# Last routing unit of a two-block transformer kernel: four V rows added by VectorE, buffers taken in another order, next weights loaded and split one block sooner

## The reference, cut to what matters

```
x[t] += sum over heads h and choices k of  gate[t,h,k] * gelu(xn[t] . U[idx[t,h,k]]) * V[idx[t,h,k]]
```

## Time and profile before

| | us |
|---|---|
| median of three runs | 1544.4 |
| lowest, highest run | 1544.03, 1548.16 |
| the profiled execution | 1549.62 |
| its span on the core | 1547.8 |
| TensorE busy in the span | 1387.3 |
| VectorE busy | 1032.8 |
| ScalarE busy | 707.7 |
| GpSimd busy | 622.3 |
| HBM read | 409.93 MB, 268 GB/s over the span |

### The profile page before, as it was taken

The page is one execution under the profiler, slowest core; times in us unless marked ns, Lnnn a source line. Parts: engine busy times, 40 slices in busy tenths (PEclk is TensorE's granted clock), DMA queues, the critical chain, the costliest instruction groups (busy, mean ns, idle before and its releaser), DMA issues.

```text
span 1547.8 us, 18260 instructions
## 1 busy us (share of the span) xinstructions
PE 1387.3 (90%) x5985; PEld 971.1 (63%) x5985; DVE 1032.8 (67%) x1923; ACT 707.7 (46%) x1374; POOL 622.3 (40%) x581
## 2 busy tenths in 40 slices
PE   7989979777787877787779999999999999999998
PEld 6877964333333333233335879788888788888887
DVE  5895787666666666666663548569863586498733
ACT  5534633233322333333334373477654745776534
POOL 2330777433333433333362521045442612364414
PEclk9999989999999999989999999899999999999999
DMA  9286699999999999999999500557665443476650
GB/s 319 82 143 224 217 333 411 421 422 421 422 423 421 421 422 422 422 421 422 422 413 348 200 29 35 164 163 210 196 211 178 159 142 108 121 207 194 216 193 28
DMA packets 187077, 415.00 MB, mean 268 GB/s; under 512 B 9883, under 2 KB 113923, under 8 KB 160387
## 3 DMA queue, kind: packets, MB, share of 16 engines
q0 software_dynamic: 43776, 268.45, 42.3%
q1 hardware_dynamic: 143090, 145.66, 30.6%
q10 hardware_dynamic: 144, 0.04, 0.0%
HBM read 409.93 MB, written 4.19 MB: 268 GB/s over the span
## 4 chain that ended last, share of the span: by engine, by line
PE 51%; DMA 21%; DVE 9%; POOL 7%; ACT 6%; issue 5%; ACTq 0%; POOLq 0%; DVEq 0%
DMA expert_rows<-in_peer_uv,route_idx 15%; PE ps L2548 10%; PE ps L2379 9%; PE ps L2092 7%; PE ps L2094 7%; PE ps L2093 7%; DMA scratch<-in_peer_uv,route_idx 5%; PE ps L2549 5%; DVE weights_lo L443 2%; POOL weights_lo L591 2%; POOL expert_rows L642 2%; ACT weights_hi L436 1%; POOL expert_rows L674 1%; PE ps L2057 1%; POOL expert_rows L661 1%
## 5 line engine op out<-in xcount | busy, mean ns | idle before, releaser
L1672 DVE CUSTOM_DVE_ANT_0 expert_rows<-expert_rows,ps 128x1024 f32<-128x1024 f32 x184 | 224.1, 1220 | 142.6 <-DMA expert_rows<-in_peer_uv,route_idx 131.6
L591 POOL TENSOR_TENSOR weights_lo<-weights_raw,weights_hi 128x512 fp32r<-128x512 f32 x120 | 159.6, 1366 | 374.5 <-ACT weights_hi L436 332.5
L2379 PE MATMUL ps<-expert_rows,scratch 128*128 128x512 f32 x512 | 241.9, 629 | 58.3 <-ACT scratch L981 58.3
L674 POOL DMA_INDIRECT expert_rows<-in_peer_uv,route_idx x156 | 148.3, 951 | 229.7 <-PE ps L2379 193.4
L436 ACT CAST weights_hi<-weights_raw 128x2048 fp32r<-128x2048 f32 x98 | 185.5, 1917 | 105.5 <-PE ps L2094 80.3
L2379 PEld LDWEIGHTS ps<-expert_rows,scratch 128*128 128x128 f32 x512 | 100.6, 201 | 198.6 <-issue 118.9
L2548 PE MATMUL ps<-x_normT,weights_hi 128*128 128x512 f32 x640 | 222.5, 393 | 0.0
L443 DVE TENSOR_TENSOR weights_lo<-weights_raw,weights_hi 128x2048 fp32r<-128x2048 f32 x68 | 160.5, 2366 | 74.4 <-ACT weights_hi L436 74.1
L967 ACT ACTIVATE proj<-proj 128x4 f32<-128x4 f32 x64 | 13.2, 206 | 402.1 <-DVE proj L1672 402.1
L2092 PE MATMUL ps<-weights_hi,x_normT 128*128 128x512 f32 (+1 forms) x496 | 188.1, 379 | 9.9 <-DVE weights_lo L443 4.2
L2094 PE MATMUL ps<-weights_hi,x_normT 128*128 128x512 f32 (+1 forms) x496 | 184.8, 372 | 0.0
(11 more groups left out here) (364 smaller groups left out, 2462.3 us busy)
## 6 DMA issues: line engine op xcount, KB each, us to landing
weights_raw<-in_ffn_up SPq DMA_DIRECT2D x88, 512.0 KB, 5.0
weights_raw<-in_ffn_down SPq DMA_DIRECT2D x22, 1024.0 KB, 4.9
weights_raw<-in_ab_w_in SPq DMA_DIRECT2D x14, 1024.0 KB, 5.7
weights_raw<-in_w_in SPq DMA_DIRECT2D x12, 1024.0 KB, 7.5
weights_raw<-in_ple_gate SPq DMA_DIRECT2D x8, 1024.0 KB, 6.2
weights_raw<-in_c_w_in SPq DMA_DIRECT2D x6, 1024.0 KB, 6.0
weights_raw<-in_w_out SPq DMA_DIRECT2D x4, 1024.0 KB, 12.7
weights_raw<-in_peer_w_query SPq DMA_DIRECT2D x4, 1024.0 KB, 12.4
```

Source lines behind the costliest of these rows:

```text
L591: ins = pool.tensor_tensor(w.lo[:, c], w.raw[:, c], w.hi[:, c].bitcast(F32), ALU.subtract)
L674: nc.gpsimd.indirect_dma_start(out=dst, out_offset=None, in_=table, in_offset=bass.IndirectOffsetOnAxis(ap=r_idx[:, q, n:n + 1], axis=0)). ...
L1672: ins = nc.vector.tensor_tensor_reduce(out=rows, in0=rows, in1=tokens, scale=1.0, scalar=0.0, op0=ALU.mult, op1=ALU.add, accum_out=r_dot[: ...
L2379: ins = pe.matmul(PS[:, (J[f"peer_{t}"] + m) % 8, :], DIAG[b][:, k, :], rows[:, m * BANK:(m + 1) * BANK], start=False, stop=False, skip_gr ...
```

## The change

In the last unit the blocks take their buffers in the order 1, 2, 0, 3 instead of 0, 1, 2, 3 (`last_buf`, `last_no`), and POOL's waits follow. The first block thus lies in the raw slots and the second in the high and low areas of slots 0 and 1. SyncE loads ab 0 and 1 when the first block is summed, ScalarE casts them when the second is summed, and VectorE no longer waits for `rows_summed` there. TensorE sums three blocks of the last unit; for the fourth no diagonal matrices are written, and VectorE adds the four V rows times their weights to x_res of tile 1, one after the other, after it has split ab 0 and 1 and ahead of the residual. ScalarE (cast of ab 2) and POOL (its splits) wait for these four additions. Apart from this, ScalarE's sigmoid raises `h_log` in place of `h_sig`, and VectorE waits for `h_log` 2.

```diff
@@ -296,6 +296,9 @@
+        LAST_BLOCKS = (1, 2, 0, 3)
+        last_buf = [pair_buf[4 * b + k] for b in LAST_BLOCKS for k in range(4)]
+        last_no = [4 * b + k for b in LAST_BLOCKS for k in range(4)]
@@ -512,7 +515,7 @@
-            sp.wait_ge(sem("rows_summed"), 4 * UNITS - 2)
+            sp.wait_ge(sem("rows_summed"), 4 * UNITS - 3)
             for p in halves(0):
                 load("ab", p)
@@ -694,12 +697,12 @@
                 for b in range(5):
                     if b < 4:
-                        pool.wait_ge(sem("rows_summed"), u * 4 + b - 3)
+                        pool.wait_ge(sem("rows_summed"), u * 4 + LAST_BLOCKS[b] - 3)
                         for n in range(4 * b, 4 * b + 4):
-                            gather(pair_buf[n][:, 0:D], a["peer_u"][0], q, n, pair_loaded[n])
+                            gather(last_buf[n][:, 0:D], a["peer_u"][0], q, n, pair_loaded[last_no[n]])
                     if b > 0:
                         for n in range(4 * b - 4, 4 * b):
-                            gather(pair_buf[n][:, D:2 * D], a["peer_v"][0], q, n, v_loaded[n])
+                            gather(last_buf[n][:, D:2 * D], a["peer_v"][0], q, n, v_loaded[n])
@@ -712,7 +715,8 @@
-            pool.wait_ge(sem("rows_summed"), 4 * UNITS)
+            pool.wait_ge(sem("rows_summed"), 4 * UNITS - 1)
+            pool.wait_ge(sem("rows_added"), 4)
             for p in (2, 3, 5, 7, 9, 11, 13):
                 split("ab", p)
@@ -986,7 +990,8 @@
                 for b in range(4):
                     weights(u, q, b)
-                    diag(u, b)
+                    if not (last and b == 3):
+                        diag(u, b)
@@ -1016,11 +1021,12 @@
-            act.wait_ge(sem("rows_summed"), 4 * UNITS - 1)
+            act.wait_ge(sem("rows_summed"), 4 * UNITS - 2)
             for p in halves(0):
                 split("ab", p)
             sqrt_table()
-            act.wait_ge(sem("rows_summed"), 4 * UNITS)
+            act.wait_ge(sem("rows_summed"), 4 * UNITS - 1)
+            act.wait_ge(sem("rows_added"), 4)
             split("ab", 2)
@@ -1040,7 +1046,7 @@
-            nc.scalar.activation(hKK, hf, ACT.Sigmoid, scale=-1.0).then_inc(sem("h_sig"), 1)
+            nc.scalar.activation(hKK, hf, ACT.Sigmoid, scale=-1.0).then_inc(sem("h_log"), 1)
@@ -1665,6 +1671,9 @@
+                elif isinstance(u, int) and u == UNITS - 1:
+                    rows = last_buf[n][:, 0:D]
+                    v.wait_ge(pair_loaded[last_no[n]], u * 16 - 16)
@@ -1734,9 +1743,14 @@
             vec_unit(UNITS - 1, 1, finish=False, start=False)
-            v.wait_ge(sem("rows_summed"), 4 * UNITS - 1)
             for p in halves(0):
                 split_lo(v, "ab", p)
+            v.wait_ge(sem("weights_ready"), 4 * UNITS)
+            for k in range(4):
+                n = 12 + k
+                v.wait_ge(v_loaded[n], 48)
+                step(nc.vector.scalar_tensor_tensor(out=X[:, 1, :], in0=last_buf[n][:, D:2 * D], scalar=r_wt[:, 1, k:k + 1],
+                                                    in1=X[:, 1, :], op0=ALU.mult, op1=ALU.add), "rows_added")
             for m in range(2):
                 residual(J["peer_1"] + m, 1, m)
@@ -1750,8 +1764,7 @@
-                v.wait_ge(sem("h_log"), 1)
-                v.wait_ge(sem("h_sig"), 1)
+                v.wait_ge(sem("h_log"), 2)
@@ -2363,7 +2376,7 @@
-                for b in range(4):
+                for b in range(3 if last else 4):
@@ -2374,7 +2387,7 @@
-                        rows = vbuf[n] if early else pair_buf[n][:, D:2 * D]
+                        rows = vbuf[n] if early else (last_buf if last else pair_buf)[n][:, D:2 * D]
```

## The result

The changed kernel takes 1551.99 us (median of 11 runs, 1546.12 to 1554.01) against 1547.30 for the kernel before (11 runs, 1544.03 to 1550.18). The ratio is 1.0025, 95% interval 1.0016 to 1.0035: about 4 us slower (4.7 us between the two medians). The interval excludes 1, so the change is a small loss; its middle lies within the 0.3% that I had set as the bound of "no change", its upper end just above it. The profiled execution took 1552.29 us with a span of 1550.5.

What follows compares the result with a forecast made beforehand. The prediction took the chain from the last V row through ab 2 to ab 3, not TensorE's row sums, as the bound. +0.85 us (ab 3) and +1.7 us (clock), summed as +2.5, on 1544.4 gave 1546.9 us, range 1540.5 to 1551.5.

Steps and rivals of the forecast that it cites:

- The likeliest case: Whole kernel: the ab 2 to ab 3 chain replaces the removed block; 1546.9 us likeliest; chance of staying within 0.3% 0.78.
- the chain from the last V row through ab 2: SyncE to POOL: the last V row's landing sets ab 2's load, its cast, norm_hi, then the cast of ab 3.
- The 6.9 us taken from TensorE are not on the path any more: TensorE, last unit: removing one block's row sums saves nothing on the path; sum up to there +0.85 us.
- four gathers, a gap, 28 back to back, the last at 826.1: POOL, last unit: a gap of 5 us after four gathers, the last gather issued 9.9 us later than before.
- The last V row at 837.0, bounds 831.9 and 839.0: DMA, last unit: last V row lands at 831.9 + 5.1 for the early loads = 837.0, against 835.5 before.
- ab 2 at 842.5: SyncE: ab 2, loaded after the last V row, lands 5.4 us later at 842.5, 1.5 us later than the cast before.
- x at 840.5: VectorE: after splits, additions and residual, the first half of x is ready at 840.5 against 842.4 before, 1.9 us gained.
- Rival 2: VectorE: additions slow, 2.30 us each, so they and not ab 2 decide; up to +7.9 us, 1552.3; chance 0.16.
- a microsecond of wait at worst: TensorE, third block of the last unit: waiting for its last V rows costs at most a microsecond; banks closed at 833.0.
- the low half of ab 3 (855.35): TensorE, third ab tile: it goes on with ab 3's low half at 855.35 instead of 854.51, +0.85 us.
- the second tile's own start: TensorE, second ab tile: starts at 846.8 against 846.4 before, behind the cast of ab 2, norm_hi and norm_lo.
- 1.7 us as the middle between 0 and 3.4: TensorE clock: new idle gaps make a 6.8 us half-clock stretch likely, costing 0 to 3.4 us; 1.7 us taken.

Runs made afterwards that it cites:

- e1: Changed kernel with buffer order, loads and casts of ab 0 and 1 put back, only the additions kept: 1562.91 us, ratio 1.0040 to the kernel before.
- f3: e1 with VectorE's four additions moved ahead of the two splits: 1558.37 us, ratio 1.0000 to the kernel before.
- e4: Changed kernel with SyncE's loads of ab 0 and ab 1 a block later again: 1570.56 us, ratio 1.0084 to the kernel before.
- f0: The changed kernel itself, unaltered, as control on the second chip: 1567.50 us, ratio 1.0061 to the kernel before.
- f2: Changed kernel with filler matmuls on TensorE ahead of the third block and the second ab tile: 1570.53 us, ratio 1.0077 to the kernel before.
- g2: Changed kernel with 32 zero matmuls on TensorE ahead of each of the last two units: 1556.24 us, ratio 1.0061 to the kernel before.
- e2: Kernel before with only the new buffer order; TensorE sums all four blocks, loads as before: 1565.88 us, ratio 1.0058 to the kernel before.
- e3: Changed kernel without the additions: new order and early loads, TensorE sums all four blocks: 1565.11 us, ratio 1.0064 to the kernel before.
- f1: Changed kernel with ScalarE's norm_hi of tile 1 ahead of the cast of ab 2: 1570.77 us, ratio 1.0080 to the kernel before.
- g1: The kernel before, unaltered, profiled a second time, on the third chip: 1545.58 us in its one run.

## Why the prediction was right, and where its steps were off

The likeliest case, no change beyond 0.3%, held by the ratio: 1.0025 on the 1544.4 us of the three runs shown gives 1548.3, against 1546.9 forecast. The medians themselves stand higher: before was 1547.3 over 11 runs, and the changed kernel's 1551.99 is half a microsecond above the end of the range. The mechanism, the chain from the last V row through ab 2, is the one that the traces show; two of its sizes were too small. That the forecast +2.5 us lies so near the 2.7 us between the two spans is luck: at the second tile the delay is 5.9 us, and a half-clock stretch that one profile of before has and the other has not hides part of it. Point by point:

- **"The 6.9 us taken from TensorE are not on the path any more"**: right, by the chain from the last V row to ab 2. e1 and f3 show it without the new order: with 16 matmuls fewer the time was 0.4% longer and the same.
- **POOL** (four gathers, a gap, 28 back to back, the last at 826.1): 826.29. Right.
- **The last V row at 837.0, bounds 831.9 and 839.0**: it landed at 839.8, past the upper bound. This is the step that failed in size, in both of its terms. I took 5.8 us for a gather alone. In the changed kernel a V gather ahead of the loads took 6.45 us, and since gathers are issued 1.24 us apart and land 1.28 us apart even with no load under way, the time to landing grows by 0.86 us over the 23 gathers up to the last: 7.3 us alone. And I took 5.1 us for the two early loads, their DMA time. While they are under way the rows land about 2.0 us apart, which puts 6.2 us in front of the last one. Together 13.5 us instead of 10.9. Why 2.1 MB hold the rows up for 6.2 and not 5.1 us is open.
- **ab 2 at 842.5**: 845.23, the same 2.8 us late. The length of its load was right (5.4 us forecast, 5.3 measured); the whole error comes from the last V row. (The forecast had SyncE's first load at 815.4; it was issued at 813.0.)
- **VectorE**: splits done at 834.7, measured 836.3 (ab 1 landed at 832.0, not 830.4); additions 5.1 us, measured 5.24; x at 840.5, measured about 842.2. Rival 2's price of 2.30 us each is refuted: 1.28 to 1.29 us in all nine traces with additions. Its mechanism, though, is real: in e1, e4, f0, f2 and g2 ScalarE's cast of ab 2 begins within 0.1 us of the end of the additions, which late splits had held up.
- **TensorE**: "a microsecond of wait at worst" at the third block was wrong. It waited 4.01 us and did eight of the sixteen matmuls at half clock, so it came to close its banks at 838.8 and not 833.0. It cost nothing only because x was late too.
- **Which wait comes last**: I named the low half of ab 3 (855.35). It was the second tile's own start: forecast 846.8, measured 849.53. The low half of ab 3 was ready at 852.93 + 5.01 = 857.9, and TensorE, 36 matmuls after the start of the second tile, came to ab 3 at 860.5. Both hang on ab 2, so the late V row moved both, and the earlier of the two places decided.
- **The clock**: 1.7 us as the middle between 0 and 3.4. The stretch came, 848.34 to 855.16, on uncovered work: the first dozen matmuls of the tile are 0.43 us apart instead of 0.23, and from the tile's start to VectorE's evacuation of it are 8.4 us instead of 5.6, 2.8 us more.

Together: 2.5 forecast, 2.7 for the tile's start, 1.1 for the clock, less 0.4 because ab 3 no longer counts, make +5.9 at the second tile, which is what was measured. What of it is seen at the end depends on the clock stretch at 972 to 982.

- **The Trainium skill**, page "DMA: Bandwidth & Descriptors", section "Anatomy of one DMA — SWDGE (gpsimd) path", would give, as an estimate, 3.2 us for a gather of 0.52 MB and a stage that ends earlier. The V gather of the changed kernel ahead of the loads took 6.5 us, has 5.8, and the shortest in the last unit, the U gather issued at 792.73 after POOL's gap, took 4.5; the measurement decides against the figure here.

## What to carry to other kernels

Before work is taken off an engine, follow the load that is queued behind the same event: here SyncE's wait for the last gather fed a cast, a norm and a tile, and the saved matmuls ran in parallel with it. An order that delays the first gathers uses up the queue's backlog (here 15 to 19 us from issue to landing became 6.5); once that is gone, loads moved forward push the last row back, here by 6.2 us for 5.1 us of DMA time. The place of short work in a queue decides its price: four additions behind two splits cost 0.4% on one chip, and ahead of them nothing on another.

## What the runs showed of the hardware that I had not expected

- **TensorE idle with no wait named.** In six profiles on two chips TensorE issued one matmul every 2.1 to 2.8 us, 3.7 to 7.3 us of idle time in all, with no semaphore named, while gathers filled the DMA engines (share 1.03 in e4 from 830 to 840); SyncE's first load was 6 to 20 us late in the same profiles. With the old order, on the second of these chips, f3 has it 2.6 us late, so part of this may belong to the chips and not to the order. The Trainium skill, page "Runtime: NRT & Kernel Launch", section "Instruction fetch mechanics", says that code is fetched by DMA in blocks of 256 instructions while the last one runs. The traces have packets of 16 KB on an instruction queue (q8). In e2, e3 and f0 one begins inside the stall (at 843.44, 836.13 and 835.35); in e4 and f1 it begins 0.8 and 1.1 us behind its end, in f2 at 827.77, before it, and the changed kernel has one at 832.56 and no stall. So the cause is open.
- **A lagging sixteenth.** The semaphore of a gather is raised in 16 steps. In g1 a gather's last sixteenth lands 2.0 us behind the fifteenth (820.2 and 822.2), and 3.2 us for the last row (831.9 and 835.1); in the changed kernel, whose gathers pause at 785 to 792, it is 2.2 us for the four gathers ahead of the pause, 0.1 to 0.2 us for nearly all behind it, and 0.9 us for the last five. It looks like a backlog of one engine that a pause clears; no run isolates it.
- **A clock stretch that comes or not.** Two profiles of the same kernel before differ by 2.9 us at one place (granted clock 0.70 and 1.00 over 968 to 985): against the one with the stretch the changed kernel's 5.9 us at the second tile are 2.7 at the end, against g1 its 7.1 us are 6.7. The 2.9 us are more than half of the 4.7 us between the medians. The windows of the profile that the prediction used, and of g1:

```profile
968.00:985.00 17.00, 15.77 (x70) 11.28 (x69) 13.32 (x15) 8.98 (x9) 1.81 (x2) 0.70 0.84 248
```

```profile
968.00:985.00 17.00, 14.79 (x85) 11.01 (x86) 15.26 (x17) 9.20 (x11) 0.69 (x1) 1.00 0.86 248
```
